# Bias bands of a two-block transformer: from a reversing product on TensorE to a VectorE add fused with the maximum

## The reference, cut to what matters

```python
bias = rel_bias_heads(rel_table, dist, head_lo, n_heads)   # table row of the distance's bucket
s = jnp.einsum("...qe,...ke->...qk", q, k) * SCALE + bias
s = jnp.where(valid, s, NEG)
m = jnp.max(s, axis=-1)
p = jnp.exp(s - m[..., None])
o = jnp.einsum("...qk,...ke->...qe", p, v)
```

## Time and profile before

| | us |
|---|---|
| median of 3 runs | 3693.66 |
| the profiled execution | 3690.75 |
| its span | 3688.9 |
| TensorE busy | 3519.9 (95% of the span) |
| GpSimd busy | 2028.1 (55%) |
| VectorE busy | 1584.2 (43%) |
| ScalarE busy | 967.4 (26%) |
| mean granted TensorE clock | 0.972 |

### The profile page before, as it was taken

One profiled execution on the slowest core, in us unless ns is written; L12 is line 12 of the kernel. 1 busy time (PEld: TensorE's weight loads), 2 busy tenths in 40 slices (PEclk: granted clock), 3 DMA queues, 4 the chain that ended last, 5 costly groups with the idle time before them and its releaser, 6 DMA issues.

```text
span 3688.9 us, 46978 instructions
## 1 busy us (share of the span) xinstructions
PE 3519.9 (95%) x18682; PEld 2895.3 (78%) x18682; DVE 1584.2 (43%) x2756; ACT 967.4 (26%) x2041; POOL 2028.1 (55%) x1216
## 2 busy tenths in 40 slices
PE   7999988999999999899999999999999999999999
PEld 6876677877779988768877787888769777878887
DVE  7844541234873221574455314331472555224430
ACT  2235434122202110221344312220121454212210
POOL 4565353553559987645433365665545332565655
PEclk9999999888999999899999999999999999999999
DMA  7533122322764443332211222332322111232323
GB/s 287 201 129 95 62 94 80 105 90 68 246 218 149 148 132 123 117 109 75 75 52 52 69 90 88 97 92 91 115 69 90 54 58 46 90 93 86 97 84 105
DMA packets 109867, 389.24 MB, mean 106 GB/s; under 512 B 12057, under 2 KB 16537, under 8 KB 108242
## 3 DMA queue, kind: packets, MB, share of 16 engines
q1 hardware_dynamic: 89280, 315.10, 26.6%
q10 hardware_dynamic: 20370, 71.13, 5.5%
HBM read 379.86 MB, written 6.32 MB: 105 GB/s over the span
## 4 chain that ended last, share of the span: by engine, by line
PE 85%; DVE 8%; ACT 3%; issue 2%; POOL 2%; DMA 1%; ACTq 0%; DVEq 0%; SPq 0%
PE ps L362 20%; PE ps L364 20%; PE ps L363 20%; PE ps L1462 3%; PE ps L1474 2%; PE ps L483 2%; PE ps L485 2%; PE ps L484 2%; PE ps L1022 2%; PE ps L1442 1%; POOL wlo L2521 1%; PE ps L1174 1%; PE ps L379 1%; DVE ada L1933 1%; DVE junk L1933 1%
## 5 line engine op out<-in xcount | busy, mean ns | idle before, releaser
L2519 POOL CAST whi<-raw 128x1024 fp32r<-128x1024 f32 (+1 forms) x606 | 619.5, 1022 | 1600.0 <-DMA raw<-in_w 1599.5
L2521 POOL TENSOR_TENSOR wlo<-raw,whi 128x1024 fp32r<-128x1024 f32 (+1 forms) x606 | 1421.6, 2346 | 48.5
L362 PE MATMUL ps<-hhi,whi 128*128 128x512 f32 x1928 | 776.1, 403 | 20.3 <-DVE q L1545 8.6
L364 PE MATMUL ps<-hhi,wlo 128*128 128x512 f32 x1928 | 761.8, 395 | 0.0
L363 PE MATMUL ps<-hlo,whi 128*128 128x512 f32 x1928 | 759.5, 394 | 0.0
L362 PEld LDWEIGHTS ps<-hhi,whi 128*128 128x128 f32 x1928 | 364.8, 189 | 108.9 <-DVE q L1545 9.4
L363 PEld LDWEIGHTS ps<-hlo,whi 128*128 128x128 f32 x1928 | 364.8, 189 | 85.8 <-issue 6.7
L364 PEld LDWEIGHTS ps<-hhi,wlo 128*128 128x128 f32 x1928 | 364.5, 189 | 80.1
L362 PE MATMUL ps<-chi,whi 128*128 128x256 f32 x816 | 239.4, 293 | 0.3 <-POOL wlo L2521 0.3
L363 PE MATMUL ps<-clo,whi 128*128 128x256 f32 x816 | 232.7, 285 | 0.0
L364 PE MATMUL ps<-chi,wlo 128*128 128x256 f32 x816 | 232.4, 285 | 0.0
(11 more groups left out here) (412 smaller groups left out, 6677.3 us busy)
## 6 DMA issues: line engine op xcount, KB each, us to landing
raw<-in_w SPq DMA_DIRECT2D x574, 512.0 KB, 3.6
ada<-in_ada ACTq DMA_DIRECT2D x96, 512.0 KB, 5.0
raw<-in_w SPq DMA_DIRECT2D x16, 384.0 KB, 3.4
att_toe<-toe_dram ACTq DMA_DIRECT2D x12, 256.0 KB, 3.0
raw<-in_w SPq DMA_DIRECT2D x16, 192.0 KB, 2.3
x<-in_x SPq DMA_DIRECT2D x4, 512.0 KB, 11.9
cond<-in_cc ACTq DMA_DIRECT2D x2, 1024.0 KB, 7.6
kc_dram<-kc ACTq DMA_DIRECT2D x2, 1024.0 KB, 5.1
```

What stands on the lines that cost most here:

```text
L362: nc.tensor.matmul(o, whi[:, buf, c], hi[:, k, 0:n], start=(k == 0), stop=False)
L364: mm = nc.tensor.matmul(o, wlo[:, buf, c], hi[:, k, 0:n], start=False, stop=(k == kt - 1))
L2519: nc.gpsimd.tensor_copy(whi[:, buf, 0:c], raw[:, buf, 0:c]).then_inc(slab_hi, 1)
L2521: nc.gpsimd.tensor_tensor(wlo[:, buf, 0:c], raw[:, buf, 0:c], whi[:, buf, 0:c].bitcast(F32), ALU.subtract).then_inc(slab_split, 1)
```

## The change

The rows of bias values are stored 128 times over, so that a band can be read the right way round; the reversing product and the matrix `flip` go; VectorE adds the band to the scores and takes the maximum in one instruction, and writes the sum back to PSUM.

```diff
-        toe_dram = nc.dram_tensor("toe_dram", [12, TOE], F32, kind="Internal")
+        toe_dram = nc.dram_tensor("toe_dram", [12, P, TOE], F32, kind="Internal")
...
                     o = pb(2 + t % 2, nk)
-                    if self.biased:
-                        if t == 0:
-                            pe.wait_ge(flip_loaded, 16)
-                        if i == 0:
-                            pe.wait_ge(self.toe_s[h % 2], 16 * (h // 2 + 1))
-                        c0 = k0 + (T // P - 1 - i) * P
-                        nc.tensor.matmul(o, self.flip, self.toe[:, h % 2, c0:c0 + nk], start=True, stop=False)
                     nc.tensor.matmul(o, hd["q"][:, i * P:(i + 1) * P], hd["k"][:, k0:k0 + nk],
-                                     start=not self.biased, stop=True).then_inc(self.s, 1)
+                                     start=True, stop=True).then_inc(self.s, 1)
...
             def load(self, act):
-                act.dma_start(self.flip, flip_in).then_inc(flip_loaded, 16)
                 self.load_toe(act, 0)
                 self.load_toe(act, 1)
...
                 if h >= 2:
-                    act.wait_ge(self.s, self.s0 + (h - 1) * (T // P))
-                act.dma_start(self.toe[:, h % 2, :], bass.AP(toe_dram, hd["toe"] * TOE, [[1, P], [1, T]]))\
+                    act.wait_ge(toe_rest, 16)
+                    act.wait_ge(self.mx, self.mx0 + (h - 1) * (T // P))
+                act.dma_start(self.toe[:, h % 2, :], bass.AP(toe_dram, hd["toe"] * P * TOE + P - 1, [[TOE - 1, P], [1, T]]))\
                     .then_inc(self.toe_s[h % 2], 16)
...
+                    if self.biased and i == 0:
+                        dve.wait_ge(self.toe_s[h % 2], 16 * (h // 2 + 1))
                     dve.wait_ge(self.s, self.s0 + t + 1)
-                    nc.vector.tensor_reduce(mx, pb(2 + t % 2, nk), AX_X, ALU.max).then_inc(self.mx, 1)
+                    o = pb(2 + t % 2, nk)
+                    if self.biased:
+                        c0 = k0 + (T // P - 1 - i) * P
+                        nc.vector.tensor_tensor_reduce(o, o, self.toe[:, h % 2, c0:c0 + nk], 1.0, -FLT_MAX, ALU.add, ALU.max,
+                                                       mx).then_inc(self.mx, 1)
+                    else:
+                        nc.vector.tensor_reduce(mx, o, AX_X, ALU.max).then_inc(self.mx, 1)
...
                     act.wait_ge(self.rw, 1)
-                    act.dma_start(toe_dram.ap(), self.row[:, :]).then_inc(self.st, 16)
+                    for lo, hi, done in ((0, 2, self.st), (2, 12, toe_rest)):
+                        act.dma_start(toe_dram.ap()[lo:hi], self.row[lo:hi, :].unsqueeze(1).to_broadcast([hi - lo, P, TOE]))\
+                            .then_inc(done, 16)
```

More of the change, by code:

```diff
@@ L89, in program @@
 def program(nc, rows, w, ada_in, x_in, xc_in, mem_in, cc_in, cols_in, cst_in, rel_in, onehot_in, toe_mask_in, lam_in,
-            rope_in, tri_in, flip_in, sgu_in, out):
+            rope_in, tri_in, sgu_in, out):
     with ExitStack() as ctx:
@@ L175, in program @@
         sgu_loaded = [sem("sgu_loaded0"), sem("sgu_loaded1")]
-        flip_loaded = sem("flip_loaded")
+        toe_rest = sem("toe_rest")
         tri_loaded = sem("tri_loaded")
@@ L1096, in program, with __init__ @@
         class SoftmaxHeads(Part):
-            def __init__(self, heads, biased, pbuf, ptbuf, toe=None, flip=None, ready=(), clear=()):
-                self.heads, self.biased, self.pbuf, self.ptbuf, self.toe, self.flip = heads, biased, pbuf, ptbuf, toe, flip
+            def __init__(self, heads, biased, pbuf, ptbuf, toe=None, ready=(), clear=()):
+                self.heads, self.biased, self.pbuf, self.ptbuf, self.toe = heads, biased, pbuf, ptbuf, toe
                 self.ready_qkv, self.clear = ready, clear
@@ L1240, in vector @@
                     hd = self.heads[h]
-                    _, nk = self.keys(t)
+                    k0, nk = self.keys(t)
                     mx = small_s[:, t % 4:t % 4 + 1]
+                    if self.biased and i == 0:
+                        dve.wait_ge(self.toe_s[h % 2], 16 * (h // 2 + 1))
                     dve.wait_ge(self.s, self.s0 + t + 1)
-                    nc.vector.tensor_reduce(mx, pb(2 + t % 2, nk), AX_X, ALU.max).then_inc(self.mx, 1)
+                    o = pb(2 + t % 2, nk)
[5 more added lines that the diff above has]
+                        nc.vector.tensor_reduce(mx, o, AX_X, ALU.max).then_inc(self.mx, 1)
                     dve.wait_ge(self.mx, self.mx0 + t + 1)
@@ L2163, in program @@
         softmax = SoftmaxHeads(heads, True, p_at[0:2], p_at[2:4], zone("att_toe", [P, 2, T], 158),
-                               zone("att_flip", [P, P], 162)[:, :], ready=all_free(values[2]),
+                               ready=all_free(values[2]),
                                clear=[lambda: (ada_used, 2 * ADA_TILES)])
@@ L2666, in _constants @@
     tri = np.stack([np.where(a < b, 0.0, NEG), np.where(a >= b, -1.0, 0.0)], 1).astype(np.float32)
-    flip = np.ascontiguousarray(np.eye(P, dtype=np.float32)[::-1])
-    return dict(cst=cst, flip=flip, onehot=onehot, toe_mask=mask, rope=rope, tri=np.ascontiguousarray(tri))
+    return dict(cst=cst, onehot=onehot, toe_mask=mask, rope=rope, tri=np.ascontiguousarray(tri))
 def _arrays(i):
@@ L2695, in _arrays @@
     out["tri"] = k["tri"]
-    out["flip"] = k["flip"]
     sw = i["sgu_w_2"].transpose(0, 3, 1, 2)
@@ L2701, in _arrays @@
     return rows, {n: np.ascontiguousarray(a) for n, a in out.items()}
-_ORDER = ["w", "ada", "x", "xc", "mem", "cc", "cols", "cst", "rel", "onehot", "toe_mask", "lam", "rope", "tri", "flip",
+_ORDER = ["w", "ada", "x", "xc", "mem", "cc", "cols", "cst", "rel", "onehot", "toe_mask", "lam", "rope", "tri",
           "sgu"]
```

## The result

The changed kernel takes 3734.1 us (median of 4 runs, 3728.15 to 3745.16) against 3690.05 us before: the ratio is 1.0118, 95% interval [1.0083, 1.0153], 44 us slower. The forecast was 3703 with a range to 3725: the sign was right, the time too low by 31 us and outside the range.

The account below looks back on a forecast made before the run. TensorE was taken to bound the kernel, the attention partly by latency through VectorE. Product -16, add +1.5 and store stall +24 made +9.5 us: 3700, or 3703 against the median; 8-in-10 range 3675 to 3725.

Parts of the forecast that it names:

- The mechanism: First projection: modulation tile loads from 76.39 us wait behind the store in ScalarE's queue; tile 22, due at 93.1, comes late.
- The rule named there: Store: spread over the largest number up to 16 dividing the slowest dimension, here 2 and 10 engines; +10 us in all.
- the store's time: ScalarE's queue, first projection: most loaded engine moves 655,360 B, so the store takes 40.5 us; tile 22 lands at 120.5.
- The rival: Store: four neighbouring partitions share one engine's 23.0 GB/s, 57 us; VectorE stands still 44 us, +26.6, 3720; chance 0.26.
- 27 us forecast for VectorE's gap: First projection: VectorE stands still 27 us for tile 22; wrong if the gap is under 5 us or over 40.
- - 4 + 1.1: After the modulation: 4 us hidden by slack before the context's norm, 1.1 us lost to TensorE's clock; 24 us in all.
- one dip of 2.5 us: TensorE after its long pause: clock granted 0.50 for 2.5 us, 1.1 us lost.
- The product: First attention: dropping the 48 bias products, 28.8 us on TensorE, gains 16 us, between 12 and 28.8.
- The add's 1.5 us: First attention, VectorE: fused add as long as the maximum, only the accumulator read of 82 ns new; 1.5 us, ends 0 and 9.
- the 29 that I had named as a sign: First attention: with L1152 gone, TensorE's busy time was to be about 29 us less.
- the first bands are there in time: First attention: VectorE's wait for the band costs nothing; first two bands issued at about 110 us, used at 178.
- The share of DMA engines: First projection: a stretch of some 30 us with the DMA engines far less busy than their 78%.

Follow-up runs that it names:

- the run with the add alone: Changed kernel with the 30 KB store and band loads of before, so the bias is added upside down: 3678.99 us, 0.9972 of the kernel before.
- the run with one row a store: Changed kernel with twelve 128-fold stores of one row each instead of two stores of two and ten rows, same bytes: 3804.11 us.

## Why the prediction was wrong

**The mechanism was right.** The tile loads stand behind the store, tile 22 is the first one late, it was due at 93.1 us (the instruction before it started at 92.05), ScalarE's copies pass the delay on. The rule named there, a store on as many engines as its outer dimension has entries, is borne out: 12.4% of the 16 engines busy for ScalarE's queue from 80 to 88 us is two engines, 59.5% from 100 to 110 is nearly ten.

**The step that failed is the store's time**, "the most loaded one moves a row of the first store and one of the second, 655,360 B: 28.5 us / 0.703 = 40.5". It took 65 us (79.3 to 144.7). The engine was not the limit: four rows in neighbouring partitions share 25.3 GB/s, so four rows need 327,680 x 4 / 25.3 GB/s = 51.8 us, and the issue of the second store, held up by the first, ended only at 88.7. 88.7 + 51.8 = 140.5, and the tail lasts to 144.7. The rival had the shared partitions, with 57 us from 78 on, a gap of 44 us and a time of 3720; it too was short, by the late issue and the clock. I gave it 0.26 since no row of before could show it; the Trainium skill, which states it, should have had more weight than the absence of a row. Term: 27 us forecast for VectorE's gap, 54.5 measured.

**Slack and clock.** "- 4 + 1.1" became + 5: the first score product is 59.6 us late for a gap of 54.5. The slack of 3.4 us before the context's norm didn't help; that wait is now 7.9 us, as TensorE, not VectorE, came last. It works from 181.4 to 198.5 us at a granted 0.50; by the share of the clock that is missing, my estimate of the cost is 0.5 x 17.1 = 8.5 us. I had allowed for one dip of 2.5 us. What made the clock stay down so long there, with TensorE busy all the time, no run shows.

**The product.** 16 us less 1.5 forecast; 10.6 in the profile, 7.5 by the run with the add alone. The add's 1.5 us fit the 1.2 measured, which the spread hides; that is partly luck, as its read of the accumulator took 142 ns and not 82. Of the product's 28.8 us, 8.5 went into longer waits for L1229 (26.2 against 17.7). Some 7 can be laid to the clock by estimate: a granted 0.92 for 0.94 over 360 us. That would leave 13, of which the profile shows 10.6; the rest is open. For the same reasons TensorE's busy time fell by 19 us and not by the 29 that I had named as a sign. That each shortened step ends in a wait, and each wait brings a slower stretch, is read from these columns and not tested by itself.

**The rest.** That the first bands are there in time held. The share of DMA engines fell as said (to 0.59), by less than I meant: an engine that waits for a partition counts as busy (93% busy for 31 GB/s in the run with one row a store).

## What to carry to other kernels

Before a large transfer is put into a queue, find out what stands behind it and how far ahead that is loaded (here 15 us), and ask from how many partitions it is read: 3.93 MB at the 368 GB/s of all engines would be 10.7 us, and it took 65. To repeat a small table many times, store it once and repeat it from DRAM, with the copy number as the outer dimension. A product that feeds an engine already waiting for another is worth the margin at that wait, step by step, and somewhat less.

## What the runs showed of the hardware

- Source rows in 12 neighbouring partitions leave SBUF at 76 GB/s together, one row or two at 26 to 27, whether 2 or 16 engines carry them. Rows on 48 partitions, which lie in part 32 apart, left at 205 GB/s while alone, rows on 96 at 337.
- An issue can last: 11.6 us for the second store and 23.8 us for the tile load behind it, with 0.33 usual. The engine does nothing else meanwhile.
- The clock doesn't follow busy time at once: in the changed kernel it was granted 0.50 for 17.1 us in which TensorE was busy without a break; the last pause, of 2.6 us, had ended 1.1 us before.
